# Seven block products for the values and gate of a retention head, in a new order of the head's work

## The reference, cut to what matters

```python
hproj = x @ w_in                       # q 256, k 256, v 512, gate 512 columns a head
q = rope(q); k = rope(k) * 256 ** -0.5
scores = (q @ k.T) * decay             # causal, in blocks of 128 tokens
o = scores @ v
o = (o - mean) * rsqrt(var + 1e-5)     # over the head's 512 columns
y += (o * silu(gate)) @ w_out          # the four heads side by side, then one product
```

## Time and profile before

| what | value |
|---|---|
| median of three runs | 1414.13 us (1412.3 to 1415.89) |
| the profiled execution, its own time | 1414.12 us |
| its span in the profile | 1412.3 us |
| PE busy | 1393.4 us, 99% of the span |
| DVE / ACT / POOL busy | 65% / 49% / 27% |
| TensorE's granted clock, mean | 0.997 of 2.4 GHz |
| the four heads | from 0 to about 318 us |
| one head in steady state | 77.8 us |

### The profile page before, as it was taken

One profiled execution on the slowest core, in us unless ns is written; L12 is line 12 of the kernel. 1 busy time (PEld: TensorE's weight loads), 2 busy tenths in 40 slices (PEclk: granted clock), 3 DMA queues, 4 the chain that ended last, 5 costly groups with the idle time before them and its releaser, 6 DMA issues.

```text
span 1412.3 us, 19358 instructions
## 1 busy us (share of the span) xinstructions
PE 1393.4 (99%) x7412; PEld 1203.4 (85%) x7412; DVE 919.2 (65%) x1562; ACT 698.8 (49%) x1131; POOL 388.2 (27%) x192
## 2 busy tenths in 40 slices
PE   9999999999999999999999999999999899999998
PEld 7888888888889888888888888778888899998887
DVE  6444354549961865545544479946877878789896
ACT  4323232236554533443443356648956465666554
POOL 5334254541034343343334230035314100000000
PEclk9999999999999999999999999999999999999999
DMA  7257946946533988975796557353122576446552
GB/s 292 90 194 204 296 155 164 263 115 258 188 103 129 289 235 221 312 176 157 210 302 161 162 207 284 135 193 126 64 83 75 165 184 173 128 173 213 197 187 111
DMA packets 53890, 260.26 MB, mean 184 GB/s; under 512 B 5568, under 2 KB 10304, under 8 KB 28224
## 3 DMA queue, kind: packets, MB, share of 16 engines
q1 hardware_dynamic: 37152, 163.04, 33.3%
q0 software_dynamic: 5760, 41.95, 14.9%
q10 hardware_dynamic: 10912, 54.40, 11.3%
HBM read 252.03 MB, written 91.23 MB: 243 GB/s over the span
## 4 chain that ended last, share of the span: by engine, by line
PE 89%; DVE 7%; ACT 2%; POOL 1%; issue 1%; DMA 0%; SPq 0%; DVEq 0%; ACTq 0%; POOLq 0%
PE bank L567 23%; PE bank L569 23%; PE bank L568 23%; PE bank L1176 6%; PE bank L1238 4%; PE bank L1127 3%; PE bank L1155 1%; DVE wlo L2082 1%; DVE wlo_a L2082 1%; DVE xlo L2082 1%; DVE br_lo L2082 1%; PE bank L1318 0%; PE bank L913 0%; PE bank L1015 0%; DMA stage<-in_w 0%
## 5 line engine op out<-in xcount | busy, mean ns | idle before, releaser
L724 POOL TENSOR_TENSOR wlo<-stage,whi 128x1024 fp32r<-128x1024 f32 (+2 forms) x116 | 291.9, 2543 | 544.8 <-ACT whi L1458 544.8
L1458 ACT ACTIVATE whi<-stage 128x1024 fp32r<-128x1024 f32 (+2 forms) x120 | 122.2, 1069 | 87.3 <-PE bank L569 64.3
L567 PE MATMUL bank<-xhi,whi 128*128 128x512 f32 (+1 forms) x428 | 149.3, 349 | 3.2 <-DVE xlo L2082 1.8
L569 PE MATMUL bank<-xhi,wlo 128*128 128x512 f32 (+1 forms) x428 | 148.5, 347 | 0.0
L568 PE MATMUL bank<-xlo,whi 128*128 128x512 f32 (+1 forms) x428 | 148.3, 346 | 0.0
L1461 ACT ACTIVATE whi<-stage 128x1024 fp32r<-128x1024 f32 (+2 forms) x125 | 118.0, 989 | 40.3 <-PE bank L569 29.4
L2082 DVE TENSOR_TENSOR wlo<-stage,whi 128x1024 fp32r<-128x1024 f32 x108 | 123.4, 1168 | 14.7 <-ACT whi L1461 14.7
L567 PEld LDWEIGHTS bank<-xhi,whi 128*128 128x128 f32 x428 | 81.1, 189 | 13.5 <-issue 2.2
L567 PE MATMUL bank<-whi,xhi 128*128 128x512 f32 (+1 forms) x236 | 91.4, 387 | 1.1 <-POOL wlo L724 1.1
L569 PE MATMUL bank<-whi,xlo 128*128 128x512 f32 (+1 forms) x236 | 90.4, 383 | 0.0
L568 PE MATMUL bank<-wlo,xhi 128*128 128x512 f32 (+1 forms) x236 | 90.3, 383 | 0.0
(11 more groups left out here) (451 smaller groups left out, 3943.5 us busy)
## 6 DMA issues: line engine op xcount, KB each, us to landing
stage<-in_w SPq DMA_DIRECT2D x79, 1024.0 KB, 4.9
tsum<-in_w ACTq DMA_DIRECT2D x32, 1024.0 KB, 14.5
stage<-tsum SPq DMA_DIRECT2D x32, 1024.0 KB, 4.8
tsum<-in_w POOLq DMA_DIRECT2D x16, 1024.0 KB, 10.1
tsum<-tsum POOLq DMA_DIRECT2D x16, 1024.0 KB, 10.1
stage<-in_w SPq DMA_DIRECT2D x8, 1152.0 KB, 6.3
usum<-in_w POOLq DMA_DIRECT2D x8, 1024.0 KB, 9.9
stage<-usum SPq DMA_DIRECT2D x32, 256.0 KB, 3.8
```

The lines of the kernel that those rows point to most:

```text
L567: pe.matmul(dst, a_hi, b_hi, start=start, stop=False)
L569: return pe.matmul(dst, a_lo, b_hi, start=False, stop=stop)
L724: pool.tensor_tensor(lo[:, r], stage[p % 2][:, r], hi[:, r].bitcast(F32), ALU.subtract).then_inc(w_lo, 1)
L1458: act.activation(parts(p)[0][:, r], stage[p % 2][:, r], ACT.Copy).then_inc(w_hi, 1)
```

## The change

The weights of v and gate of one head are seen as a 2 by 2 grid of blocks: rows 0 to 511 and 512 to 1023 by v and gate columns. B11 and B21 are v's two row blocks, B12 and B22 the gate's. x is cut likewise into tokens 0 to 255 and 256 to 511 by 512 columns. Winograd's form of Strassen's scheme then needs seven products of 24 matmuls in place of eight: with B11, B21, B22 and four sums T1 = B12 - B11, T2 = B22 - T1, T3 = B22 - B12, T4 = B21 - T2.

- TensorE: q and k stay as they are (48 matmuls each). v and gate take 7 x 24 = 168 matmuls where they took 192. The order in a head becomes: B11, k, B21, scores, B22, T1, T2, T3, T4, `scores @ v`, q of the next head, transposes. Products of 24 matmuls follow one another with two buffer pairs, as panels of 48 did.
- Weights: 9 splits a head in place of 6. GpSimd makes the remainders of q, k, B11, B21, B22 and T3 (6 a head, as before), VectorE those of T1, T2 and T4. VectorE also makes the four sums of weights, 128x2048 each.
- Sums of x: four of 128x1024 with their rounded parts and remainders, once, inside head 0, on VectorE and ScalarE.
- Results: v and gate come out with tokens on partitions. VectorE combines the products with twelve additions of 128x512 a head out of PSUM, ScalarE copies two intermediate results out (`kept1`). The normed output is multiplied by the gate before it is transposed (one instruction), ScalarE scales it by the inverse deviation, and after the transposes ScalarE copies it to `oT`.
- Loads: 6 a head, into stages of their own; B21's stage in heads 1 to 3 is the gate's buffer, free when the head before is normed, and B12's load stands behind it in SP's queue and waits for GpSimd's remainder of k.
- Weight sums of AO: the same transfers, in other places: GpSimd starts four of the accumulations after B22 of head 1, two after B22 of head 2, two after B11 of head 3; ScalarE's copies are started after T2's rounding in heads 1, 2 (4 transfers) and 3 (8), and after head 0 (4). The load of x for the residual moves from the start to head 3.
- Between the heads and AO: the last head's transposes come after AO's second step.

The core of the diff (between the parts shown stand the scores, `scores @ v` and VectorE's additions, gate products and remainders, told above), TensorE:

```diff
-            def rest(h, n):
...
-                token_tiles(A0 + 3, n, 4, 4, lambda q: A[q][:, :], False, True, nothing, a_v)
...
-                pe.wait_ge(a_qklo, 4 * h + 4)
...
+            def head(h):
+                if h:
+                    pe.wait_ge(a_c, 12 * h)
+                block_product(h, A_B11, X)
+                turned_product(h, AK)
+                pe.wait_ge(a_k1, 2 * h + 2)
+                block_product(h, A_B21, X, True)
+
+                pe.wait_ge(a_qklo, 4 * h + 4)
+                if h:
+                    pe.wait_ge(a_ot, 4 * h)
+                for kt in S_ORDER:
...
+                pe.wait_ge(a_vlo, 4 * h + 2)
+                if h == 0:
+                    pe.wait_ge(vs_l, 4)
+                block_product(h, A_B22, X)
+                block_product(h, A_T1, Y)
+                pe.wait_ge(a_dec, 4 * h + 2)
+                block_product(h, A_T2, Z)
+                pe.wait_ge(a_dec, 4 * h + 4)
+                block_product(h, A_T3, W)
+                pe.wait_ge(a_c, 12 * h + 6)
+                block_product(h, A_T4, X)
...
+            for h in range(HA):
+                head(h)
+                if h + 1 < HA:
+                    pe.wait_ge(a_c, 12 * h + 10)
+                    turned_product(h + 1, AQ)
+                    turn_head(h)
             for d in range(13):
...
+                if d == 2:
+                    turn_head(HA - 1)
```

VectorE, the first part of a head:

```diff
+            def head(h):
+                s0, s1, s2 = a_stage[2], a_stage[1], a_stage[0]
...
+                def t1():
+                    dve.wait_ge(a_ld[1], 32 * h + 32)
+                    dve.wait_ge(g_plo, 12 * h + 4)
+                    dve.tensor_tensor(s0, s1, s0, ALU.subtract).then_inc(g_sum, 1)
+
+                def t3():
+                    dve.wait_ge(a_ld[0], 32 * h + 32)
+                    dve.tensor_tensor(s1, s2, s1, ALU.subtract).then_inc(g_sum, 1)
...
+                rope(h, 0)
+                rope_lo(h, 0)
+                if h == 0:
+                    operand_sum(0)
+                    operand_sum(1)
+                    operand_sum_lo(0)
...
+                    operand_sum(2)
+                    operand_sum_lo(1)
...
+                    operand_sum(3)
+                    operand_sum_lo(2)
+                t1()
+                if h:
+                    t3()
+                rope(h, 1)
+                rope_lo(h, 1)
+                if h == 0:
+                    operand_sum_lo(3)
+                for q in range(2):
+                    v_low(q, X[q][:, :])
...
+                both(A_T1)
...
+                dve.tensor_tensor(s0, s2, s0, ALU.subtract).then_inc(g_sum, 1)
...
+                both(A_T2)
...
+                dve.tensor_tensor(s0, a_staged(h, A_B21), s0, ALU.subtract).then_inc(g_sum, 1)
+                dve.wait_ge(a_m, 7 * h + 5)
...
+                both(A_T4)
+                dve.wait_ge(a_m, 7 * h + 6)
...
+                dve.wait_ge(a_m, 7 * h + 7)
...
```

```diff
+                head_hi(h, A_B22, (a_ld[0], 32 * h + 32), (a_qk, 4 * h + 4))
+                for m in range(2, 4):
+                    act.wait_ge(a_q32, 4 * h + (m + 1))
+                    copy(qk_hi[:, m, :], work[:, m % 2 * 2, :], a_qkhi)
```

More of the change, by code:

```diff
@@ L336, in program @@
         a_on = sem("a_on")
+        a_m = sem("a_m")
         a_t = sem("a_t")
@@ new lines, in turned_product @@
+            def turned_product(h, j):
+                wh, wl = [w.rearrange("p (k n) -> p k n", k=KX) for w in a_parts(h, j)]
+                if h and j == AK:
+                    pe.wait_ge(a_ot, 4 * h - 2)
+                for m in range(2):
+                    c = slice(m * P, (m + 1) * P)
+                    for k in range(KX):
+                        if m == 0 and k in (0, KX // 2):
+                            head_need(h, j, k > 0)
+                        last = split_dots(pe, (W if j == AQ else Y)[m][:, :], wh[:, k, c], wl[:, k, c], xhi[:, k, :],
+                                          xlo[:, k, :], k == 0, k == KX - 1)
+                    last.then_inc(a_qk, 1)
@@ new lines, in block_product @@
+            def block_product(h, j, banks, onto=False):
+                wh, wl = [w.rearrange("p (k n) -> p k n", k=PK) for w in a_parts(h, j)]
+                x_hi, x_lo = a_operand(j)
+                for kk in range(PK):
+                    if kk % 2 == 0:
+                        head_need(h, j, kk > 0)
+                    for a in range(2):
+                        r = slice(a * P, (a + 1) * P)
+                        last = split_dots(pe, banks[a][:, :], x_hi[:, kk, r], x_lo[:, kk, r], wh[:, kk, :], wl[:, kk, :],
+                                          kk == 0 and not onto, kk == PK - 1, onto)
+                last.then_inc(a_m, 1)
@@ L1650, in head @@
[L1650 to L1657 removed]
+                    act.wait_ge(a_ot, 4 * h)
+                    operand_hi(AO, 0)
@@ L1677, in head, with turned_out @@
-                tanh(2)
-                tanh(3)
-                if not last:
-                    split_hi(A0 + 1, a_g, 4 * h + 8, PAN, 6 * h + 6)
+                for q in range(TT):
+                    act.wait_ge(a_on, 4 * h + q + 1)
+                    copy(onorm[:, q, :], onorm[:, q, :], a_sc, small[:, 2, q:q + 1])
+            def turned_out(h):
+                for j in range(VT):
+                    act.wait_ge(a_t, 4 * h + j + 1)
+                    copy(oT[:, 4 * h + j, :], B[j][:, :], a_ot)
@@ new lines, in rope_lo, with head_lo @@
+            def rope_lo(h, a):
+                for m in range(2):
+                    dve.wait_ge(a_qkhi, 4 * h + (2 * a + m + 1))
+                    lo_of(qk_lo[:, 2 * a + m, :], work[:, 2 * m, :], qk_hi[:, 2 * a + m, :], a_qklo)
+            def head_lo(h, j, b):
+                hi, lo = a_parts(h, j)
+                r = slice(b * PAN // 2, (b + 1) * PAN // 2)
+                dve.wait_ge(g_hi, 2 * (SPLITS * h + j) + b + 1)
+                lo_of(lo[:, r], a_staged(h, j)[:, r], hi[:, r], g_dlo)
```

484 lines of the change are left out of this document (313 added, 171 removed).

## The result

The kernel after takes 1449.76 us (median of 4 runs, 1449.66 to 1451.35), the kernel before, on the same chip, 1413.86 (4 runs, 1412.3 to 1415.89). The ratio is 1.0256, 95% interval [1.0238, 1.0273]: 2.6% slower. The forecast was slower too, but 1422 us within 1400 to 1436: +8.1 was worked out, +35.9 came.

What follows compares the result with a forecast made beforehand. It took TensorE, busy 99% of the span, as the bound. From 1414.1 us, -21.8 (matmuls) +12.8 (scores' wait) +6.1 (head 0) +1.0 (head 1) +4 (head 3's end) +6 (clock) = +8.1: 1422 us, range 1400 to 1436.

Steps and rivals of the forecast that it cites:

- What is removed: TensorE, heads: 24 matmuls fewer in each head, 96 in all at 0.2267 us, -21.8 us.
- The wait for the scores, head 0 and head 1: TensorE waits for k's remainders: 3.2 us in each head (+12.8), +6.1 more in head 0, +1.0 for head 1's load.
- Hidden at no cost: Other roundings, scaling, copies, most loads and the moved accumulating transfers lie under TensorE's work: no time added.
- The end of head 3: ScalarE's eight starts delay T3's rounding about 2 us, then remainders and norm queue up: +4 us, bounds 0 and 6.
- AO: AO stays bound by TensorE; VectorE, busy 72 of 76 us there, keeps up: no time added.
- The clock: TensorE's clock falls after four stalls, 2.5 us for the first and 1.2 each other: +6, bounds 0 and 12.
- The short chain: Rival: GpSimd not in the rope's way, chain behind k's product 5.3 us against 5.44, 1396 us; chance 0.15.
- The waits with a full clock: Rival: TensorE's waits come but its clock stays, 1411 us; chance 0.3.
- Everything slips: Rival: one more VectorE turn before two products a head, 8 to 16 us more, 1430 to 1438; chance 0.1.
- the prediction's own sign of being wrong: Wrong if scores start within 1 us of B21's end, or TensorE waits mostly for weight remainders T1 to T4.

Runs made afterwards that it cites:

- qkfirst: The kernel after with ScalarE rounding k's two parts before B22 instead of after it: 1462.31 us, 1.0343 of before.
- two: The kernel after with the edits of `spread` and `qkfirst`, and ScalarE's eight starts of head 3 moved behind B21's rounding: 1419.19 us, 1.0028 of before.
- later: The kernel after with VectorE's sums T1, T3 (head 0: also one sum of x, one remainder) behind the second rope: 1449.85 us, 1.0253 of before.
- all: `two` with VectorE's sums T1 and T3 behind the second rope, as in `later`: 1434.65 us, 1.0145 of before.
- four: `five` with VectorE's order second rope, v's remainders, T1's sum, T3's last, and two sums swapped in head 0: 1429.38 us, 1.0107 of before.
- t3dve: The kernel after with T3's remainder made by VectorE instead of GpSimd, transfers left in place: 1442.12 us, 1.0192 of before.
- spread: The kernel after with GpSimd's accumulating transfers started one at a time, behind separate remainders and AO's first two steps: 1437.52 us, 1.0163 of before.
- three: `two` with two of ScalarE's four copies after head 0 moved behind head 1's T1 rounding, accumulating transfers one place later: 1414.36 us, 0.9997 of before.
- three_t3: `three` with T3's remainder made by VectorE, the edit of `t3dve`: 1414.22 us, 1.0008 of before.
- warm: The kernel after with 145 matmuls, whose result is overwritten, put into TensorE's waits: 1446.47 us, 1.0232 of before.
- five: `three` with ScalarE's eight starts of head 3 moved into AO's loop, one in each step from the fourth: 1419.95 us, 1.0035 of before.

## Why the prediction was wrong

**What is removed** (-21.8): right, see the ledger.

**The wait for the scores, head 0 and head 1** (+19.9): right, 19.2. Heads 2 and 3 had 3.0 each for 3.2, head 0 8.5 for 9.3. Heads 2 and 3 stall for the reason given, the meeting of GpSimd and VectorE: `qkfirst` takes B22 out of the rope's way and leaves 0.2 and 1.4 there, `two` 0.2 and 0.4. Head 0 has both reasons, as foretold: `qkfirst` alone leaves 6.5, `later` alone 7.3, both together (`all`, `four`) 3.2. Head 1's 4.8 for 4.2 is the load foreseen: it landed 10.20 us after its issue, and VectorE stood for it.

```profile
117.39 2.29 DVE L2655 TENSOR_TENSOR oT<-stage,oT 128x2048 f32<-128x2048 f32 x1 [8.31 <-DMA stage<-in_w]
119.60 2.29 DVE L2659 TENSOR_TENSOR stage<-stage 128x2048 f32<-128x2048 f32 x1
```

These sums of 2.29 us are the long operations that the trace of before lacked: GpSimd's pair, which met the second, took 6.44 us, and 4.77 undisturbed. That agrees with the rule of the Trainium skill ("SBUF — State Buffer", section "SBUF: two separate sides"), by which such an operation holds GpSimd for its whole length, as far as one pair shows it.

**Hidden at no cost**: this is the step that failed. It said that "the moved accumulating transfers are due only in AO". That is when their results are due. But they were put in front of T3's remainder on GpSimd's queue, four in a row, and that remainder is due one product (5.44 us) after its rounding. The prediction gave these starts no time at all; what the runs show in its place is that a start holds GpSimd until the transfer before has landed, so that the four held it from 126.38 to 157.01, 30.6 us. In the kernel before each start stood behind another panel's remainder, 8.6 us or more from the last. The trace of before had the sign, which the prediction didn't read. GpSimd in head 3, four starts with remainders between them:

```profile
261.88 0.82 POOL L749 DMA_DIRECT2D usum<-in_w  x1 [2.64 <-DMA usum<-in_w]
...
272.43 0.83 POOL L749 DMA_DIRECT2D usum<-in_w  x1 [2.32 <-DMA usum<-in_w]
275.78 4.77 POOL L724 TENSOR_TENSOR wlo<-stage,whi 128x1024 fp32r<-128x1024 f32 x2 [2.52 <-ACT whi L1458]
281.02 0.82 POOL L749 DMA_DIRECT2D usum<-in_w  x1 [0.47 <-issue]
```

Each of the three waited (2.64, 2.32, 0.47 us) though the copies that the program has them wait for had landed by 240 us, when ScalarE passed the same wait, and each came 0.3 to 0.4 us after the landing of the transfer before (261.6, 272.1, 280.7). The same gap is there, only mostly filled. The error cost 8.8 us in head 1 (`t3dve` and `spread` each take it away), part of head 3's 7.5, and the clock behind both.

**The end of head 3** (+4, bounds 0 and 6): the place was right and the size wrong, 9.0. ScalarE's starts were taken at the 5.8 of the earlier trace rows and lasted 12.2 (1.28 and 10.91), since GpSimd's transfers now ran beside them. T3's rounding was foretold 2 us late with starts of 5.8; these 6 us more make it some 8. The 1.5 at AO's third step is in every run (1.4 to 1.5), those without a late T3 too.

**AO** (counted at nothing, since VectorE "keeps up"): 3.4 us came at its end, and each of the eleven runs has 3.3 to 5.7 there for `xres`. After, and below it before:

```profile
426.36 5.65 POOL L791 TENSOR_TENSOR wlo<-stage,whi 128x1024 fp32r<-128x1024 f32 x2 [77.82 <-DVE wlo_a L2276]
426.39 3.40 DVE L2450 SCALAR_TENSOR_TENSOR xres<-oT,small,rows 128x1024 f32<-128x1024 f32 x1
...
394.50 1.28 DVE L2256 SCALAR_TENSOR_TENSOR xres<-oT,small,rows 128x1024 f32<-128x1024 f32 x1
395.78 5.75 POOL L724 TENSOR_TENSOR wlo<-stage,whi 128x1024 fp32r<-128x1024 f32 x2 [70.45 <-ACT whi L1458]
```

It is the meeting of the rope again: GpSimd's half panel begins 0.03 us ahead of VectorE's operation, which then takes 2.1 us more than before, where GpSimd came after it. That is 2.1 of the 3.4 us; no run moved this remainder, so it is read from the traces and not tried.

**The clock** (+6, bounds 0 and 12): heads 0 and 2 lost 2.4 and 1.7, 4.1 for the 3.7 counted. The other 11.2 lie in head 1, head 3 and AO, where the unforeseen waits are. Mechanism and price per stall were right, the number of stalls was not.

**The rivals.** The short chain didn't come: GpSimd was in the rope's way in every head. The waits with a full clock didn't either. "Everything slips" named 1430 to 1438 with T1 to T4 late by one turn of VectorE; weight remainders were late, but by a start of a transfer and only in two heads. By the prediction's own sign of being wrong it was close: 16.3 of the 40.7 us of idling were for T3's remainder, 19.2 for `qk_lo`. So the range was too short at its upper end because no case held a blocked queue. That the kernel got slower was foretold for reasons that came, and isn't luck.

## What to carry to other kernels

When a transfer's start is moved in an engine's queue, ask two questions: when its result is due, and what stands behind it. Several starts in a row are not several times one start: the duration shown (0.8 us) isn't what the queue pays. Give each a place of its own, with as much other work in front of the next as the transfer takes to land (7.4 to 18.5 us here), and look up that landing in the trace. A product taken out of a chain is worth its full time only while everything that lay under it still fits: here 21.8 us of matmuls were saved in every version, and the best ones (`three`, `three_t3`) gave back just as much in stalls and clock, so that no version beat the kernel before. Rows that show a short wait tell where the chain is tight, but shifting work out of it needs room elsewhere (`later`, `all`, `four`).

## What the runs showed of the hardware

- Accumulating transfers of 1 MB that GpSimd starts one after another begin 8 to 14 us apart (126.38, 134.43, 142.54, 156.45; in head 3 291.94, 300.70, 308.81, 321.35), though each start lasts 0.8 to 0.95 us and nothing in the program holds the next. Each next one begins 0.2 to 0.4 us after the one before has landed, and in 13 traces of 40 such transfers none begins earlier. Whether the landing itself releases it or something that comes with the landing isn't shown.
- Six starts of ScalarE's own transfers (512 KB each) took 4.56 us before and 5.05 in `spread`, but 10.6 to 13.9 in the five kernels where GpSimd's accumulating ones run beside them (after, `t3dve`, `qkfirst`, `later`, `warm`), and ScalarE's next rounding waited for them. Beside one accumulating transfer and B12's load, six took 9.64 in `three`. In `five`, where they stand some 3 to 8 us apart, each took 0.6 us beside the same kind of transfer. So it takes both, the row and the company; the company of other traffic alone wasn't tried.
- A load of 1 MB beside four of ScalarE's copies landed after 10.2 to 10.9 us (after, `two`, `spread`), and after 4.7 in `three`, where two of the copies had been moved away; 4.9 is the median.
- An operation of VectorE with two inputs in SBUF that meets GpSimd's half panel takes 0.9 to 2.2 us longer: 1.63 to 2.88 for 0.69 in the rope, 3.40 for 1.28 at the end of AO.
